# A hybrid decoder step on one core: in the odd layer, two heads' scores and outputs in turn on upper and lower rows, and small products in pieces between panel chunks

## What is computed

```python
def mlstm_chunk(carry, inp):
    c, n, m = carry
    q, k, v, ig, lf = inp
    b = lax.cumsum(lf, axis=2)
    dmat = jnp.where(causal, b[..., :, None] - b[..., None, :] + ig[..., None, :], -jnp.inf)
    inter = b + m[..., None]
    m_row = jnp.maximum(inter, jnp.max(dmat, axis=-1))
    w_intra = jnp.exp(dmat - m_row[..., None])
    w_inter = jnp.exp(inter - m_row)
    qk = jnp.einsum('bhtd,bhsd->bhts', q, k) * w_intra
    num = w_inter[..., None] * jnp.einsum('bhtd,bhdv->bhtv', q, c) + jnp.einsum('bhts,bhsv->bhtv', qk, v)
    den = w_inter * jnp.einsum('bhtd,bhd->bht', q, n) + jnp.sum(qk, axis=-1)
    h = num / jnp.maximum(jnp.abs(den), jnp.exp(-m_row))[..., None]
    ...
def odd_mixer(h, state0, w_in, b_i, b_f, g_out, w_out):
    proj = (h @ w_in).astype(jnp.float32)
    ...
    hh, c, n, m = mlstm(q, k, v, ig, lf, c0, n0, m0)
    hh = rmsnorm(hh, g_out.reshape(ML_HEADS, ML_DV))
    out = (hh.reshape(bsz, L, ML_WIDTH) * jax.nn.sigmoid(o)).astype(h.dtype)
    return out @ w_out, c, n, m
```

## Time and profile before

| | us |
|---|---|
| timed runs, median of 3 | 1421.23 |
| timed runs, lowest and highest | 1411.24, 1422.82 |
| the profiled execution | 1418.06 |
| its span, first to last instruction | 1416.3 |
| TensorE busy in it | 1345.2 |
| mean granted clock of TensorE | 0.971 |

### The profile page before, as it was taken

How to read it: one execution, slowest core, us unless ns; L and a number is a source line. 1 busy time by engine, 2 the same in 40 slices (tenths; PEclk the granted TensorE clock), 3 DMA queues, 4 the chain that set the end, 5 groups by cost and what they waited for, 6 DMA issues and landing times. The chain is left out here.

```text
span 1416.3 us, 25318 instructions
## 1 busy us (share of the span) xinstructions
PE 1345.2 (95%) x10450; PEld 1286.1 (91%) x10450; DVE 671.9 (47%) x950; ACT 433.9 (31%) x667; POOL 160.7 (11%) x149
## 2 busy tenths in 40 slices
PE   5678889899999999999999999999999999999998
PEld 4667666899999999999988888999999999999998
DVE  3875576564444234444553433367644433344422
ACT  5222355232222112222242444442322221222211
POOL 1573300340000000002300000004200000000000
PEclk9788799999999999999999999999999999999999
DMA  6164211153333322233221211213323332223332
GB/s 170 51 107 74 80 35 31 46 139 90 88 89 102 91 74 86 82 96 103 52 75 46 62 48 47 62 48 103 105 89 89 94 103 71 76 88 89 106 92 75
DMA packets 230634, 115.08 MB, mean 81 GB/s; under 512 B 34533, under 2 KB 226489, under 8 KB 230537
## 3 DMA queue, kind: packets, MB, share of 16 engines
q1 hardware_dynamic: 225912, 113.00, 28.4%
q10 hardware_dynamic: 4656, 1.16, 0.8%
HBM read 107.77 MB, written 7.38 MB: 81 GB/s over the span
## 5 line engine op out<-in xcount | busy, mean ns | idle before, releaser
L315 PE MATMUL ps<-xh,whi 128*128 128x272 f32 x1408 | 291.6, 288 | 2.1 <-DVE wlo L274 2.1
L315 PE MATMUL ps<-xh,wlo 128*128 128x272 f32 x1408 | 291.4, 288 | 0.0
L315 PE MATMUL ps<-xl,whi 128*128 128x272 f32 x1408 | 290.3, 288 | 0.0
L315 PEld LDWEIGHTS ps<-xh,whi 128*128 128x128 f32 x1408 | 221.5, 188 | 2.6 <-issue 2.5
L315 PEld LDWEIGHTS ps<-xl,whi 128*128 128x128 f32 x1408 | 221.2, 188 | 0.0
L315 PEld LDWEIGHTS ps<-xh,wlo 128*128 128x128 f32 x1408 | 219.8, 189 | 0.0
L274 DVE TENSOR_TENSOR wlo<-wraw,whi 128x1024 fp32r<-128x1024 f32 (+1 forms) x118 | 165.2, 1400 | 98.6 <-ACT whi L269 94.2
L269 ACT CAST whi<-wraw 128x1024 fp32r<-128x1024 f32 (+1 forms) x118 | 133.4, 1130 | 140.1 <-PE ps L315 140.1
L315 PE MATMUL ps<-hh,whi 128*128 128x272 f32 x704 | 145.8, 288 | 0.0
L315 PE MATMUL ps<-hl,whi 128*128 128x272 f32 x704 | 145.5, 288 | 0.0
L315 PE MATMUL ps<-hh,wlo 128*128 128x272 f32 x704 | 145.5, 288 | 0.0
(11 more groups left out here) (536 smaller groups left out, 1977.1 us busy)
## 6 DMA issues: line engine op xcount, KB each, us to landing
wraw<-in_w_gate SPq DMA_DIRECT2D x88, 256.0 KB, 3.0
wraw<-in_w_up SPq DMA_DIRECT2D x88, 256.0 KB, 3.1
wraw<-in_w_down SPq DMA_DIRECT2D x32, 384.0 KB, 3.8
wraw<-in_w_in_odd SPq DMA_DIRECT2D x48, 256.0 KB, 3.1
wraw<-in_w_down SPq DMA_DIRECT2D x32, 320.0 KB, 3.2
wraw<-in_w_in_even SPq DMA_DIRECT2D x20, 256.0 KB, 4.5
wraw<-in_w_out_odd SPq DMA_DIRECT2D x16, 256.0 KB, 3.1
ev_xs<-in_x_prompt SPq DMA_DIRECT2D x2, 1024.0 KB, 7.0
```

Source lines behind the costliest of these rows:

```text
L315: ins = pe.matmul(K.ps[:, 2 * s + h, 0:HT], w[s][:, k, :], a[:, k, h * HT:(h + 1) * HT], start=start, stop=stop)
```

## The change

TensorE's list, and with it ScalarE's and VectorE's, is reordered in five ways. Nothing is computed otherwise, apart from the sample outputs, where one product per head pair takes the place of one per head (lines 2488, 2489).

1. Panel 3 is finished and three chunks of panel 4 are issued ahead of the wait for the gates. VectorE evicts panel 2 and splits panel 4 between the gates' scans and their last steps; ScalarE splits panel 4 ahead of its wait for the gates.
2. Sample maxima and log weights move out of panel 4 into panel 5 and are issued in three pieces with a chunk between them. ScalarE splits panel 6 only after the maxima's Exp.
3. `scores(j)` issues both heads, alternating between upper and lower rows. Both heads' log weights come ahead of it, and VectorE masks both heads behind each other.
4. `outputs(j)` issues all products of 128 rows of both heads and then those of 64 rows, alternating between the heads. It stands where `outputs(a)` stood; `outputs(b)` one panel later is gone, and `back(a)` keeps its place behind the fourth chunk of panel p + 3.
5. The sample outputs are issued in three pieces between chunks 4 to 7 of panel 21.

```diff
@@ TensorE, ahead of the head pairs
         panel(1)
         panel(2)
-        panel(3, 0, 4)
+        panel(3)
+        panel(4, 0, 3)
         pe.wait_ge(S["gates"], 1)
...
-        panel(3, 4)
-        panel(4, 0, 4)
+        panel(4, 3, 6)
...
+        panel(4, 6)
+
+        def sample_maxima(heads):
+
+            for h in heads:
+                o = order(h) * LS
+                ins = pe.matmul(ps[:, 4, o:o + LS], selr(h), m[:, LP:T], start=True, stop=True)
+            return ins
...
-        def scores(h):
+        def scores(j):
 
-            j, two = h // 2, h % 2
-            if two:
-                pe.wait_ge(S["w"], h)
-            elif j:
-                pe.wait_ge(S["mo"], h)
+            a = 2 * j
+            pe.wait_ge(S["w"], a + 1)
+            if j:
+                pe.wait_ge(S["mo"], a)
             else:
                 pe.wait_ge(S["emt"], 1)
             for i in range(NC):
                 ts = slice(i * P, (i + 1) * P)
-                ins = pe.matmul(ps[:, 7 - two, ts], proj[rows(h), 4 + j, ts], proj[rows(h), j, ts], start=True, stop=True)
-            ins.then_inc(S["s"], 1)
+                for two in range(2):
+                    q = rows(two)
+                    ins = pe.matmul(ps[:, 7 - two, ts], proj[q, 4 + j, ts], proj[q, j, ts], start=True, stop=True)
+            ins.then_inc(S["s"], 2)
...
-        def outputs(h):
+        def outputs(j):
...
+            for two in range(2):
+                for i in range(NC):
+                    pe.matmul(dst(two, i), B.at[two][:, i * P:(i + 1) * P], B.v_nat[two][:, i, :], start=i % 2 == 0, stop=False)
+            for i in range(1, NC):
+                for two in range(2):
+                    q = rows(two)
+                    pe.matmul(dst(two, i), B.qw[q, i * P:(i + 1) * P], cn[q, i - 1, :], start=False, stop=i in (1, NC - 1))
@@ TensorE, head-pair stage
             p, a, b = 4 * j + 5, 2 * j, 2 * j + 1
-            panel(p, 0, 2)
             if j:
+                panel(p, 0, 2)
                 back(a - 1)
+            else:
+                pe.wait_ge(S["ct"], 1)
+                sample_maxima(range(4))
+                panel(p, 0, 1)
+                sample_maxima(range(4, MH)).then_inc(S["b4"], 1)
+                panel(p, 1, 2)
+                sample_log_weights()
+                panel(p, 2, 3)
             keys_by_token(j)
             inter_weights(j)
-            panel(p, 2, 4)
+            panel(p, 2 if j else 3, 4)
             log_weights(a)
-            scores(a)
-            panel(p, 4, 7)
+            panel(p, 4, 6)
+            log_weights(b)
+            panel(p, 6)
             values_by_token(a)
-            panel(p, 7)
-            panel(p + 1, 0, 2)
-            log_weights(b)
-            panel(p + 1, 2, 4)
-            scores(b)
-            panel(p + 1, 4, 6)
+            panel(p + 1, 0, 1)
+            scores(j)
+            panel(p + 1, 1, 4)
             values_by_token(b)
-            panel(p + 1, 6)
+            panel(p + 1, 4)
             panel(p + 2, 0, 1)
             states(j)
             panel(p + 2, 1, 5)
-            outputs(a)
+            outputs(j)
             sample_scores(j)
             panel(p + 2, 5)
-            panel(p + 3, 0, 1)
-            outputs(b)
+            panel(p + 3, 0, 2)
             sample_values(j)
-            panel(p + 3, 1, 4)
+            panel(p + 3, 2, 4)
             back(a)
             panel(p + 3, 4)
@@ TensorE, sample outputs in panel 21
-        for h in range(MH):
-            o, two = order(h), h % 2
-            dst = ps[:, 6, o * LS:(o + 1) * LS]
-            pe.matmul(dst, B.io[:, h // 2, :], K.ident[0:2 * LS, two * LS:(two + 1) * LS], start=True, stop=False)
-            pe.matmul(dst, B.v_s[:, h, :], B.at_s[:, o, :], start=False, stop=True)
+        both = ps[:, 6, 0:2 * P].rearrange("p (two j t) -> p two j t", two=2, j=4)
+        for j in range(4):
+            pe.matmul(both[:, :, j, :], B.io[:, j, :], K.ident[0:2 * LS, 0:2 * LS].rearrange("p (two t) -> p two t", two=2),
+                      start=j == 0, stop=False)
+        panel(21, 4, 5)
+        for part in range(2):
+            for o in range(4 * part, 4 * part + 4):
+                pe.matmul(ps[:, 6, o * LS:(o + 1) * LS], B.v_s[:, o % 4 * 2 + o // 4, :], B.at_s[:, o, :],
+                          start=False, stop=o == MH - 1)
+            panel(21, 5 + part, 6 + part)
...
-        panel(21, 4)
-        panel(22, 0, 1)
+        panel(21, 7)
+        panel(22, 0, 2)
@@ VectorE, head-pair stage
-            masked(a)
...
-            panel_end(p)
+            evac(p)
+            masked(a)
+            masked(b)
+            split_lo_of(dve, p + 2)
             scaled_keys(a)
-            masked(b)
             scaled_keys(b)
             panel_end(p + 1)
```

More of the change, by code:

```diff
@@ L2309, in _, with sample_log_weights @@
         ins.then_inc(S["b5"], 1)
-        pe.wait_ge(S["ct"], 1)
-        for h in range(MH):
[L2312 to L2320, removed]
+        panel(4, 6)
[4 more added lines that the diff above has]
+            return ins
+        def sample_log_weights():
+            for h in range(MH):
+                o = order(h) * LS
+                pe.matmul(ps[0:LS, 6, o:o + LS], selr(h, 0, LS), rr[:, LP:T], start=True, stop=True)
+            pe.wait_ge(S["c_in"], 32)
+            pe.transpose(ps[:, 6, 2 * P:2 * P + LS], B.n0_nat[:], K.ident[0:LS, 0:LS]).then_inc(S["b6"], 1)
         def keys_by_token(j):
@@ L2394, in states, with dst @@
                     ins.then_inc(S["dc"], 1)
-        def outputs(h):
-            j, two = h // 2, h % 2
+        def outputs(j):
             pe.wait_ge(S["at"], 2 * j + 2)
[L2400 to L2406, removed]
+            pe.wait_ge(S["cn"], NC * j + NC)
+            def dst(two, i):
+                return ps[:, (4 if two else 6) + i // 2, (i % 2) * (DV + 1):(i % 2 + 1) * (DV + 1)]
+            for two in range(2):
[5 more added lines that the diff above has]
+                    pe.matmul(dst(two, i), B.qw[q, i * P:(i + 1) * P], cn[q, i - 1, :], start=False, stop=i in (1, NC - 1))
         def back(h):
@@ L2506, in _ @@
         ins.then_inc(S["dn"], 1)
-        panel(22, 1)
+        panel(22, 2)
         panel(23, 0, 2)
@@ L2560, in _ @@
         split_hi_of(act, 3)
+        split_hi_of(act, 4)
         act.wait_ge(S["gates"], 1)
@@ L2563, in _ @@
         act.copy(B.rh[:], rr[:, 0:LP]).then_inc(S["parts"], 1)
-        split_hi_of(act, 4)
+        split_hi_of(act, 5)
         act.wait_ge(S["em_pe"], 1)
@@ L2572, in _ @@
                        bias=B.ln_eps[:]).then_inc(S["ems"], 1)
+        split_hi_of(act, 6)
         act.wait_ge(S["wts"], 3)
         act.activation(B.wt_s[:], B.wt_s[:], ACT.Exp).then_inc(S["wte"], 1)
-        split_hi_of(act, 6)
         def weights(h):
@@ L2626, in _ @@
             weights(a)
+            weights(b)
             values(a)
             split_hi_of(act, p + 2)
-            weights(b)
             values(b)
@@ L2730, in _ @@
             st(dve.tensor_tensor_scan(m[:, ts], lf[:, ts], ig[:, ts], m0[:, n:n + 1], ALU.add, ALU.max), s)
+        panel_end(2)
         st(dve.memset(mp[:, 0:1], 0.0), s)
@@ L2742, in _ @@
                           mp[:, 0:NC].unsqueeze(2).broadcast_to([MH, NC, P]), ALU.add).then_inc(S["gates"], 1)
-        panel_end(2)
         dve.wait_ge(S["parts"], 4)
         dve.tensor_tensor(B.rl[:], rr[:, 0:LP], B.rh[:].bitcast(F32), ALU.subtract).then_inc(S["parts"], 1)
+        panel_end(3)
         dve.wait_ge(S["ct_pe"], 1)
@@ L2754, in _ @@
         dve.tensor_copy(B.wi_s[:].rearrange("p j x -> p (j x)"), ps[:, 5, 0:P]).then_inc(S["sgate"], 1)
+        panel_end(4)
         dve.wait_ge(S["b6"], 1)
```

3 lines of the change are left out of this document (removed).

## The result

| | before | after |
|---|---|---|
| timed runs side by side, median (us) | 1419.34 | 1413.63 |
| lowest and highest | 1409.04, 1423.85 | 1408.32, 1418.35 |
| number of runs | 20 | 20 |
| the profiled execution | 1418.06 | 1413.94 |
| its span | 1416.3 | 1411.7 |

The ratio is 0.9964, with a 95% interval of 0.9950 to 0.9977: 5.7 us less, where 12.1 were forecast. That is within 1% of no change, and 0.6 us above the range. In this comparison the kernel before is at 1419.34, not at the 1421.2 of its first three runs.

A forecast was written before the change was run, and what follows sets the result against it. TensorE, busy 95% of the span, was taken as the bound through its stream, waits and clock. From the profiled 1418.1 us, -4.8 - 1.8 - 4.7 - 5.2 - 9.8 + 10.2 + 4.0 = -12.1 gave 1406.0 us, range 1397 to 1413.

The forecast's parts named there:

- Gates: Gates' transposes after panel 3: the 3.2 us wait and 1.6 us of half clock go, -4.8 us.
- Sample maxima: Maxima and log weights in pieces: 2.5 us saved if the clock holds, 0.7 for ways in and out, -1.8 us.
- Scores: Four head-pair stages: both heads' scores overlap on the row halves in 1.3 us, 4 x -1.3 = -5.2 us.
- Rival 3: Scores and outputs: row halves don't overlap, a pair costs two records, 1.7 us more a stage, 1413 us; chance 0.07.
- Outputs and the wait at back(a): Head-pair stages: outputs in turn save 4 x -2.4 = -9.8 us; back(a) comes too early and waits, 4 x +2.6 = +10.2.
- Rival 1: No new wait at back(a), as the chain runs under something unseen; 1391.8 us, chance 0.10.
- The clock behind that wait: Behind back(a)'s new waits: two of four followed by half clock at 2.0 us each, +4 us; bounds 0 to 10.
- Rival 4: Clock falls at every back(a) and stays low long, 5.1 us a time, 20.4 instead of 4.0; 1422.4 us, chance 0.08.
- sample outputs: Sample outputs in pieces in panel 21: 2.7 us saved on products, 2.0 on half clock behind them, -4.7 us.
- rival 2: Small products in pieces with one chunk between still let the clock fall, at maxima and sample outputs; 1410.5 us, chance 0.15.
- the clock's part: Half clock saved at gates 1.6, maxima 2.5 and sample outputs 2.0 us, against +4.0 for falls behind back(a)'s waits.

The follow-up runs named there:

- e1: The changed kernel with 21 unused products of 272 columns filling TensorE's wait ahead of back(a); 1404.42 us, ratio to before 0.9893.
- e7: e3 and e4 together: the changed kernel with later back(a) and back(b) and two chunks between the sample outputs' pieces; 1392.73 us, ratio to before 0.9820.
- e10: The same kernel as e3 in a second set of runs, beside e9; 1393.92 us, ratio to before 0.9812.
- e12: The changed kernel with 14 unused products in panel 1, shifting what follows in the odd layer by 1.75 us; 1412.31 us, ratio to before 0.9929.
- e2: The changed kernel with outputs head by head in their old places again, scores still in turn; 1404.03 us, ratio to before 0.9891.
- e3: The changed kernel with back(a) four chunks later and back(b) two chunks later; 1394.56 us, ratio to before 0.9834.
- e4: The changed kernel with two panel chunks instead of one between the sample outputs' pieces; 1411.14 us, ratio to before 0.9949.
- e5: The kernel before with only the changes to gates, sample maxima with log weights, and sample outputs; 1406.47 us, ratio to before 0.9914.
- e8: e7 with more chunks between the pieces of sample maxima and log weights too; 1394.82 us, ratio to before 0.9824.
- e9: e3 with each head's outputs by itself and in its old place, as in e2; 1404.69 us, ratio to before 0.9890.
- e11: The changed kernel with 7 unused products in panel 1, shifting what follows in the odd layer by 0.88 us; 1417.95 us, ratio to before 0.9966.
- e6: The kernel before with only the head-pair stages changed (scores and outputs in turn); 1417.10 us, ratio to before 0.9982.

## Why the prediction was wrong

**Gates: right.** The wait is gone, and with it the half clock. No wait took its place.

**Sample maxima: right in size, by luck of this execution.** log_weights(a) comes 7.0 us sooner (forecast 6.6 for gates and maxima). But the clock held there in after, e1, e7, e10 and e12 and fell in e2, e3, e4, e5, e8, e9 and e11, for 6.8 to 17.1 us. With one chunk between the pieces it fell in 6 of 11 profiles, and log_weights(a) then came 2.6 to 3.8 us later than 41.16 (e11 less its shift among them). A term that I priced as certain holds in five of eleven profiles.

**Scores: right.** Two heads in 1.10 us; a stage without a fall takes 40.33 instead of 41.51, -1.2, where scores, outputs and wait together were forecast at -1.1. Rival 3 (halves that don't overlap) falls.

**Outputs and the wait at back(a): right.** 2.74 us for both heads (forecast 2.8), a wait of 2.78 (forecast 2.85). e2 shows the sum of the two: +0.1 us a stage, forecast +0.1. The chain of eviction, split, variance, two table loads and normalisation is what the wait is made of, and e3 takes it away by putting work in front of it. Rival 1 falls. The Trainium skill (TensorEngine Tiling, PSUM Bottleneck) says that copying out of PSUM may become the bound once products are packed. The trace agrees in part: the readers of the outputs did become what TensorE waits for, and those of the scores did not, as forecast. But of the 6.15 us only the eviction and the normalisation read PSUM, 0.73 and 0.69 us; the bound is a chain of dependent steps, and not the rate of copying.

**The clock behind that wait: the mechanism right, the term too small.** I took two falls of four, 4.0 us. There were three: 2.7, 1.6 and 1.4, 5.6 in all. Over the five profiles that have the wait (after, e4, e6, e11, e12) it is 14 of 20 places. It never fell in a kernel without the wait or with the wait filled. Rival 4 (half clock behind each and for long, 5.1 us a time) falls: the half clock lasts 3.4 or 6.8 us and costs 1.2 (e4) to 2.7.

**The step that failed: sample outputs, forecast -4.7, measured -1.7.** From their start to panel 25 it is 32.07 us before and 30.37 after. Where the clock held with the same code (e3, e5, e9) it is 27.39, which is the forecast to 0.1 us. So the products and their ways in and out were counted rightly; that one chunk between pieces would hold the clock was wrong. The clock fell there in after, e1, e2, e10, e11 and e12. This is rival 2 (1410.5), at one of its two places; at the other it comes true in six of eleven profiles. It was given 0.15, on the ground that the head-pair stages mix small products and chunks at 1.00 throughout; but these have more chunks to most blocks of small products than panel 21 and panel 5 now have, and the products there are larger. With two chunks the clock held in three of three (e4, e7, e8), which speaks for the distance; the size of the products was not tested.

**The sum.** In the odd layer: forecast -12.1; +3.0 for the sample outputs, +1.6 for the falls behind the wait, -0.3 for gates, maxima and the stages gives -7.8, which is what the two profiles show. The rest isn't in the odd layer: the even layer was 3.2 us longer in the profile of after, through one fall of the clock between 242 and 250 us that before's execution didn't have. In the timed runs, at full clock after lies 10.2 us below before, where the parts of my sum without the clock come to -10.0 (-3.2 + 0.7 - 2.7 - 5.2 - 9.8 + 10.2); the clock's part was forecast at -2.1 and is +3 to +6. So within the spread the whole miss is the clock. In the profiles it is 5.8 us more lost time: 1.7 of it in the odd layer (20.5 against 17.1 us at half clock), 0.7 behind TensorE's last product, where it costs nothing, and 3.4 in a layer that the change doesn't touch. I argued only from the odd layer and gave the range no room for this; the spread of the three runs shown, 11.6 us, could have told me that one kernel's runs differ by as much as the gain.

**What stays open.** By what rule the clock falls at blocks of small products with dense chunks between them, and why the even layer loses more in most executions of one kernel than of another. Profiles of the same kernel (e3, e10), and the place at 242 us in before and after, where the same products start within 0.1 us of the same time of the span, show that neither the products around the place nor their time since the start decides it alone.

## What to carry to other kernels

Speeding up a step that covers an element-wise chain turns its gain into a wait: before packing products, follow the chain that they cover and move its consumer by what is saved; here that move alone was worth 1.3% (ratios of e3 and after, 0.9834 and 0.9964) and without it the packing of the outputs nothing. An idle stretch of 2.8 us of TensorE costs itself and, in 14 of 20 cases here, another 1.2 to 2.7 us through half clock, so here it was better filled even with products that nobody needs. Compare kernels whose gain is under 1% by the layer that was changed, and by time at full clock and time lost apart, or the median mostly tells how the clock fell.

## What the runs showed of the hardware

- TensorE's clock fell to 1.2 GHz while TensorE was 100% busy with small products: at the earlier trace rows before, and in after behind pieces of 8 records of 64 or 32 columns with one chunk of 0.75 us between them (918.8 to 925.6 us). A timeline of after shows the fall in one place; the third piece of sample outputs is followed by a chunk at half clock:

```profile
915.88 1.07 PE L2506 MATMUL ps<-ml_at_s,ml_v_s 32*128 32x32 f32 x8
916.89 0.52 PE L2273 MATMUL ps<-xh,whi 128*128 128x272 f32 x2
...
917.84 1.10 PE L2506 MATMUL ps<-ml_at_s,ml_v_s 32*128 32x32 f32 x8
918.86 0.82 PE L2273 MATMUL ps<-xh,whi 128*128 128x272 f32 x2
```

- Once it had fallen at or behind the maxima it stayed low for 6.8 to 17.1 us although chunks followed, at the sample outputs for 3.4 or 6.8; behind a wait of 2.8 us with dense panels on both sides it was back after 3.4 us in 11 of 14 cases and after 6.8 in three.
- Two products on the upper and lower 64 rows start as a pair: 16 records of 128 columns took 1.10 us, as long as 8.
- Filling a wait with unused products made a kernel 9 us faster in the median and 7.1 in the odd layer (e1). Removing the wait by order made it 19 to 20 us faster in the median and 16 to 17 in the odd layer (e3, e10).
- The same products, at the same time of the span to 0.1 us, ran at 1.00 in one execution and fell to half for 6.8 us in another (236 to 250 us, before and after).
